# Attention scores as three rounded products of split queries and keys, in the softmax stages of a two-block network

## What is computed

```python
# first block, both layers: dilated attention, 8 heads of 64
scores = einsum(q, k) * d ** -0.5;  scores = where(mask, scores, -inf)
p = exp(scores - m);  o = einsum(p, v) / p.sum(-1)
# second block, second layer: differential attention, 4 heads with two maps of 64
attn = softmax(q1 @ k1 * s + bias_d) - lam * softmax(q2 @ k2 * s + bias_d);  out_d = attn @ v_d
# ... and chosen attention, 8 heads of 64 over the 256 best keys of a token, picked by an index score
out_c = softmax(where(chosen & causal, q @ k * s + bias_c, -inf)) @ v_c
```

## Time and profile before

| | |
|---|---|
| time, median of 3 runs | 3228.14 us (3226.29 to 3228.87) |
| profiled execution | 3228.16 us, of which 3226.3 us are the span of the instructions |
| PE busy | 2971.4 us (92%) |
| DVE busy | 2444.6 us (76%) |
| ACT busy | 1416.7 us (44%) |
| POOL busy | 420.5 us (13%) |
| dilated stages | 174.4 to 218.4 and 845.8 to 889.9 |
| differential, chosen stage | 2420.7 to 2483.4 and 2484.2 to 2556.0 |

### The profile page before, as it was taken

One profiled execution on the slowest core, in us unless ns is written; L12 is line 12 of the kernel. 1 busy time (PEld: TensorE's weight loads), 2 busy tenths in 40 slices (PEclk: granted clock), 3 DMA queues, 4 the chain that ended last, 5 costly groups with the idle time before them and its releaser, 6 DMA issues. The chain is left out here.

```text
span 3226.3 us, 40647 instructions
## 1 busy us (share of the span) xinstructions
PE 2971.4 (92%) x14002; PEld 2396.8 (74%) x14002; DVE 2444.6 (76%) x2663; ACT 1416.7 (44%) x1696; POOL 420.5 (13%) x249
## 2 busy tenths in 40 slices
PE   7998999999989999879979999995988979999995
PEld 6777788877777878656767888884765768888884
DVE  4566888565567996576978999996487669999996
ACT  1233211022323110163236777774336327777774
POOL 0110112211101213200000000001323100000001
PEclk9998999999989999989989999997999979999997
DMA  4242765332324663164239999994214249999994
GB/s 169 66 164 66 232 213 166 109 119 95 144 92 151 226 199 107 51 189 113 74 129 363 386 371 372 386 370 168 92 40 127 94 172 384 383 374 390 384 387 156
DMA packets 346603, 667.28 MB, mean 207 GB/s; under 512 B 21984, under 2 KB 138700, under 8 KB 338268
## 3 DMA queue, kind: packets, MB, share of 16 engines
q1 hardware_dynamic: 339708, 642.60, 56.5%
q0 software_dynamic: 6752, 22.81, 2.1%
HBM read 612.22 MB, written 53.13 MB: 206 GB/s over the span
## 5 line engine op out<-in xcount | busy, mean ns | idle before, releaser
L2924 DVE TENSOR_TENSOR expert_w_low<-expert_w_raw,expert_w_high 128x2048 fp32r<-128x2048 f32 x290 | 663.7, 2289 | 66.0 <-ACT expert_w_high L2881 65.7
L2881 ACT CAST expert_w_high<-expert_w_raw 128x2048 fp32r<-128x2048 f32 x290 | 555.0, 1915 | 192.1 <-PE bank L144 180.4
L142 PE MATMUL bank<-expert_w_high,expert_x_high 128*128 128x512 f32 x928 | 379.5, 409 | 6.5 <-DVE expert_w_low L2924 4.3
L142 PE MATMUL bank<-first_XH,first_w_high 128*128 128x512 f32 (+1 forms) x944 | 369.8, 392 | 0.0
L144 PE MATMUL bank<-expert_w_high,expert_x_low 128*128 128x512 f32 x928 | 365.3, 394 | 0.0
L143 PE MATMUL bank<-expert_w_low,expert_x_high 128*128 128x512 f32 x928 | 363.9, 392 | 0.0
L143 PE MATMUL bank<-first_XL,first_w_high 128*128 128x512 f32 (+1 forms) x944 | 363.1, 385 | 0.0
L144 PE MATMUL bank<-first_XH,first_w_low 128*128 128x512 f32 (+1 forms) x944 | 362.9, 384 | 0.0
L222 DVE TENSOR_TENSOR first_w_low<-first_w_raw,first_w_high 128x2048 fp32r<-128x2048 f32 (+2 forms) x94 | 287.1, 3054 | 3.2
L220 DVE CAST first_w_high<-first_w_raw 128x2048 fp32r<-128x2048 f32 (+2 forms) x94 | 111.7, 1188 | 173.1 <-PE bank L144 152.1
L1440 ACT ACTIVATE ffn_conv<-bank,ffn_taps 128x512 f32<-128x512 f32 x88 | 68.5, 780 | 358.4 <-PE bank L144 358.3
(11 more groups left out here) (545 smaller groups left out, 5962.1 us busy)
## 6 DMA issues: line engine op xcount, KB each, us to landing
expert_w_raw<-in_moe_w_gate_dram SPq DMA_DIRECT2D x116, 1024.0 KB, 8.4
expert_w_raw<-in_moe_w_up_dram SPq DMA_DIRECT2D x116, 1024.0 KB, 13.6
expert_w_raw<-in_moe_w_down_dram SPq DMA_DIRECT2D x58, 1024.0 KB, 13.9
modulation<-in_moe_w_down_dram SPq DMA_DIRECT2D x58, 1024.0 KB, 14.1
ffn_mod_w<-in_ada_w_dram SPq DMA_DIRECT2D x48, 1024.0 KB, 5.0
first_w_raw<-in_w_up_dram SPq DMA_DIRECT2D x88, 512.0 KB, 6.6
first_w_raw<-in_w_down_dram SPq DMA_DIRECT2D x22, 1024.0 KB, 4.8
first_w_raw<-in_w_in_dram SPq DMA_DIRECT2D x20, 1024.0 KB, 5.1
```

What stands on the lines that cost most here:

```text
L142: nc.tensor.matmul(out, rounded(st[0]), rounded(mv[0]), start=start, stop=False)
L2881: nc.scalar.copy(rounded(high[:, part_of(e, n), :]), weights.place(place)).then_inc(w_high, 1)
L2924: nc.vector.tensor_tensor(rounded(low[:, part_of(e, n), :]), weights.place(place), high[:, part_of(e, n), :], ALU.subtract).then_inc(w_spl ...
```

## The change

`ScoreParts` splits the queries and keys of a pair of heads: `round` casts both (128x512 each) on ACT, `rest` subtracts both on DVE, and `products` issues six fp32r products, alternating between the two heads' halves of the array. The first pair of the dilated stage and the first head of the differential stage keep the plain products. Each other pair is split a few units before it is used; the first pair of the chosen stage in unit 12 of the differential one. The low parts have two slots, so the two pairs whose low part has been overwritten are subtracted again (`AGAIN_AT`) and the last four units go through the pairs backwards. To make room, two of three slots of the chosen stage's bias rows move into the modulation tile, and the following phase's parts and rows move to `score_high` and to the mixed rows.

```diff
+class ScoreParts:
+    def round(self, act, h, done):
+        for n in range(2):
+            last = self.nc.scalar.copy(rounded(self.high(h)[n]), self.raw[n](h))
+        last.then_inc(done, 1)
+    def rest(self, dve, h, done):
+        for n in range(2):
+            last = self.nc.vector.tensor_tensor(rounded(self.low(h)[n]), self.raw[n](h), self.high(h)[n], ALU.subtract)
+        last.then_inc(done, 1)
+    def products(self, outs, h, width, queries, keys, stop):
+        high, low = self.high(h), self.low(h)
+        parts = ((high[0], high[1]), (high[0], low[1]), (low[0], high[1]))
+        for n, (q, k) in enumerate(parts):
+            for m, out in enumerate(outs):
+                r = width * m
+                done.append(self.nc.tensor.matmul(out, rounded(q[r:r + width, queries]), rounded(k[r:r + width, keys]), ...
...
 dilated_phase
+        SPLIT_AT = {0: 1, 2: 2, 5: 3}
...
+                if hp:
+                    pe.wait_ge(pair_split, hp)
+                    for last in parts.products(...)
...
                 for m in range(2):
                     softmax_max(i, m)
+                if i in SPLIT_AT:
+                    dve.wait_ge(pair_high, SPLIT_AT[i])
+                    parts.rest(dve, SPLIT_AT[i], pair_split)
                 if i >= 1:
                     copy(i - 1)
...
+                if i in SPLIT_AT:                       # ACT, after exp(i)
+                    parts.round(act, SPLIT_AT[i], pair_high)
                 if i >= 1:
                     copy(i - 1)
...
 chosen_attention_phase
+        SPLIT_AT = {3 * hp + 1: hp + 1 for hp in range(HEADS_C // 2 - 1)}     # units 1, 4, 7
+        AGAIN_AT = {units.index((hp + 2, TT - 1)): hp for hp in range(2)}     # units 13, 12
...
                 if i >= 1:
                     copy(i - 1)
+                if i in SPLIT_AT:
+                    dve.wait_ge(pair_high, SPLIT_AT[i])
+                    parts.rest(dve, SPLIT_AT[i], pair_split)
+                elif i in AGAIN_AT:
+                    parts.rest(dve, AGAIN_AT[i], pair_split)
...
 differential_phase
+        SPLIT_AT = {0: (parts, 1), 4: (parts, 2), 8: (parts, 3), 12: (next_parts, 0)}
...
                 if u >= 1:
                     weigh(u - 1)
+                if u in SPLIT_AT:
+                    which, h = SPLIT_AT[u]
+                    dve.wait_ge(head_high, split_number[u])
+                    which.rest(dve, h, head_split)
                 if u >= 2:
                     combine(u - 2)
```

More of the change, by code:

```diff
@@ L579, in _, with __init__, attn_score_parts @@
             V.tensor_tensor(S["KGR"][:, :], ps[k % BANKS][:, :], rest[:, :], ALU.mult).then_inc(gated, 1)
+class ScoreParts:
+    def __init__(self, nc, queries, keys, high, low):
+        self.nc, self.raw, self.high, self.low = nc, (queries, keys), high, low
+    def round(self, act, h, done):
[9 more added lines that the diff above has]
+        parts = ((high[0], high[1]), (high[0], low[1]), (low[0], high[1]))
+        done = []
+        for n, (q, k) in enumerate(parts):
+            for m, out in enumerate(outs):
+                r = width * m
+                done.append(self.nc.tensor.matmul(out, rounded(q[r:r + width, queries]), rounded(k[r:r + width, keys]),
+                                                  start=(n == 0), stop=stop and n == len(parts) - 1))
+        return done[-len(outs):]
+def attn_score_parts(nc, S, queries, keys):
+    high = lambda h: [S["score_high"][:, n, h, :] for n in range(2)]
+    low = lambda h: [S["score_low"][:, h % 2, n, :] for n in range(2)]
+    return ScoreParts(nc, lambda h: S[queries][:, h, :], lambda h: S[keys][:, h, :], high, low)
 def pair_values(V, k, h):
@@ L616, in dilated_phase @@
         zero_rows = G["consts"][:, 0:D]
+        rows_of = lambda a: (lambda hp: [a[:, 4 * n + hp, :] for n in range(2)])
+        parts = ScoreParts(nc, lambda hp: S["QA"][:, hp, :], lambda hp: S["KA"][:, hp, :], rows_of(G["XH"]), rows_of(G["XL"]))
+        pair_high = ph.sem("pair_high")
+        pair_split = ph.sem("pair_split")
+        SPLIT_AT = {0: 1, 2: 2, 5: 3}
         zero_set = ph.sem("zero_set")
@@ L3634, in chosen_attention_phase @@
         mix_bank = lambda i: ps[6 + i % 2]
+        parts = attn_score_parts(nc, S, "QC", "KC")
+        pair_high = ph.sem("pair_high")
+        pair_split = ph.sem("pair_split")
+        SPLIT_AT = {3 * hp + 1: hp + 1 for hp in range(HEADS_C // 2 - 1)}
+        AGAIN_AT = {units.index((hp + 2, TT - 1)): hp for hp in range(2)}
         block = ph.block()
@@ L3655, in scores @@
                 for m in range(2):
-                    r = HD_C * m
                     if i >= 2:
                         pe.wait_ge(max_done, 2 * (i - 2) + m + 1)
-                    nc.tensor.matmul(score_bank(i, m)[:, :], S["QC"][r:r + HD_C, hp, t * P:(t + 1) * P], S["KC"][r:r + HD_C, hp, :],
-                                     start=True, stop=False)
+                if t == TT - 1 and hp < 2:
+                    pe.wait_ge(pair_split, len(SPLIT_AT) + 2 - hp)
+                elif hp:
+                    pe.wait_ge(pair_split, hp)
+                parts.products([score_bank(i, m)[:, :] for m in range(2)], hp, HD_C, slice(t * P, (t + 1) * P), slice(0, SEQ), False)
                 if t == TT - 1:
@@ L3850, in scores @@
                         pe.wait_ge(max_done, 2 * (u - 2) + m + 1)
-                    nc.tensor.matmul(ps[2 * (u % 2) + m][:, :], S["QD"][r:r + HD_D, h, t * P:(t + 1) * P], S["KD"][r:r + HD_D, h, :],
-                                     start=True, stop=False)
+                    if h == 0:
+                        nc.tensor.matmul(ps[2 * (u % 2) + m][:, :], S["QD"][r:r + HD_D, h, t * P:(t + 1) * P], S["KD"][r:r + HD_D, h, :],
+                                         start=True, stop=False)
+                if h:
+                    pe.wait_ge(head_split, h)
+                    parts.products([ps[2 * (u % 2) + m][:, :] for m in range(2)], h, HD_D, slice(t * P, (t + 1) * P), slice(0, SEQ), False)
                 if u == 0:
@@ L3953, in _ @@
                                          accum_out=row_sum[:, u, m:m + 1]).then_inc(exp_done, 1)
+                if u in SPLIT_AT:
+                    which, h = SPLIT_AT[u]
+                    which.round(act, h, head_high)
                 if u >= 3:
@@ L4170, in second_block @@
         with ExitStack() as parts:
-            G["XH"], G["XL"] = parts.enter_context(nc.sbuf_tensor("attn_out_XH", [P, KD, SEQ], F32)), masks
-            rows = [chosen_bias.rows[:, r, :, :].rearrange("p m n -> p (m n)") for r in range(TT - 1)] + [S["Y"][:, TT - 1, :]]
+            G["XH"], G["XL"] = S["score_high"].rearrange("p r m n -> p (r m) n"), masks
+            rows = [S["Y"][:, r, :] for r in range(1, TT)] + [chosen_bias.own[:, :, :].rearrange("p m n -> p (m n)")]
             attn_out_phase(nc, G, S["Y"], w_out, mod(2), (S["QC"], rows, room[:, 3:5, :, :], S["VC"].rearrange("p m n -> p (m n)")), routers[1])
```

25 lines of the change are left out of this document (19 added, 6 removed).

## The result

3293.27 us, median of 4 runs (3288.64 to 3294.11), against 3228.51 us for the kernel before (4 runs): ratio 1.0201, interval 1.0189 to 1.0213. The change costs 65 us, where 26 were forecast; the sign was right, the size lies outside the range.

A forecast was written before the change was run, and what follows sets the result against it. DVE was taken to bind the differential stage and have little room in the chosen one, PE to bind the dilated ones. 9.6 + 6.6 + 9.0 + 1.0 = 26 us on 3228.16 gave 3254 us, range 3240 to 3268.

The forecast's parts named there:

- The bound: DVE full in the differential stage, 0.3 us a unit of room in the chosen; PE binds the dilated stages' steady part.
- the products take what was said: Scores on PE: six fp32r products run as three side-by-side pairs, 0.88 us instead of 1.06, gaining 0.18 us a unit.
- Rivals 1, 3 and 4: PE halves run serially: 3268 us, chance 0.10; DVE additions hide: 3222, 0.04; lags caught up within stages: about 3232, 0.07.
- Rival 2: PE's clock falls at each of some ten stalls, 1.7 us each: +15 us, about 3268 us; chance 0.11.
- One sentence: By the skill's weight-load rule the products' gain on PE would be nearly gone, which would not change the sum.
- Differential, +9.6 forecast: Differential stage: DVE idles 1.85 us and subtracts 1.22 us in units 4, 8 and 12, plus a start delay; +9.6 us.
- Chosen, +6.6 forecast: Chosen stage: DVE idles and subtracts 2.57 us in units 1, 4 and 7, plus a POOL meeting, less offsets; +6.6 us.
- Unit 4: Chosen stage: DVE's subtractions meet POOL's 4.54 us subtraction and wait for its end, 1.75 us more, less 0.8 us.
- the second meeting with POOL, which slides apart (0.5): Chosen stage: DVE's operation no longer meets POOL's second subtraction, taking 0.5 us off.
- DVE's delay reach PE at the mark: Chosen stage: the mark comes 7.1 us later; PE's wait for it grows from 0.85 to some 3 us.
- Dilated, +4.5 each forecast: Dilated stages: splits in units 0, 2 and 5 delay PE 5.2 us, products return 0.7; +4.5 each, both +9.0 us.
- Clock, +1 us forecast (bounds 0 to 6): Differential stage: splits leave PE idle some 2.3 us in a piece, a low clock follows; +1 us.

The follow-up runs named there:

- e2: Changed kernel without DVE's subtractions and waits for casts; all three products of a head take high parts, ACT casts behind its copy; 3227.8 us.
- e5: Changed kernel with unused filler fp32 products on PE in its longest stalls in all four stages; 3267.1 us.
- e13: Changed kernel with plain fp32 scores in both dilated stages, splits and their waits kept; 3275.8 us.
- e6: Changed kernel, but POOL zeroes the low parts of two output-weight slots in the chosen stage instead of subtracting them; 3273.5 us.
- e9: Changed kernel with DVE's subtractions a unit later and ACT's casts behind its copies, some dilated splits a unit later; 3253.3 us.
- after: The changed kernel itself, with all its splits and products, against the kernel before; 3293.27 us, ratio 1.0201.
- e12: Changed kernel with POOL's two output-weight subtractions in the chosen stage each cut into eight of 256 columns; 3279.0 us.
- e14: Changed kernel with plain fp32 scores in the first dilated stage only, splits kept; 3282.0 us.
- e15: Changed kernel with plain fp32 scores in the second dilated stage only, splits kept; 3273.9 us.

## Why the prediction fell short

The bound was read rightly: DVE's chain carries the splits in the full stages, and the products take what was said (0.89 for 0.88 us); nothing of it shows in the time (e2). Rivals 1, 3 and 4 are out by the rows above. Rival 2 named the right mechanism, with 15 us where at least 21 were; 3268 us is still short of 3293. One sentence is off by the prediction's own numbers: without the products' gain its sum would not stay as it is, but grow by 0.5 + 1.4 = 1.9 us. By steps:

- **Differential, +9.6 forecast, +14.2 measured.** DVE idled 1.73 us (1.85 said) and subtracted for 1.29. With PE filled the stage is at +10.6 (e5). The other 3.6 us are clock, as far as one can tell: the same code without fillers came as low as +11.7 (e13), with less low clock.
- **Chosen, +6.6 forecast, +16.9 measured.** Unit 4 behaved as said (2.40 us for the first subtraction). The step that failed here is "the second meeting with POOL, which slides apart (0.5)": it slid the other way, into nearly the whole of POOL's 4.53 us, and lost 3.55 us there where the kernel before had lost 0.53: 3.0 us more on DVE instead of 0.5 less. Without both blocks the stage is at +4.2 (e6). The path was wrong too. The prediction had DVE's delay reach PE at the mark, where PE waited 1.00 us and not 3, hardly more than the 0.85 before. PE stood 8.8 us instead in five waits before its turns, for a copy of ACT; in the two longest, 2.83 and 3.42 us, it came behind exponentials that had waited for DVE's late maximum.
- **Dilated, +4.5 each forecast, +15.8 and +18.2 measured.** On the good course of the clock it is +5.7 and +6.8 (e5), so this term was 1.2 and 2.3 us small, and 10.1 and 11.3 us are clock.
- **Clock, +1 us forecast (bounds 0 to 6).** This is the step that failed. In the four stages PE spent some 122 us at 0.50, by the length and the granted clock of each window (60.00 x 2 x 0.28 = 34 in the first), against 20 us before. The forecast counted a low stretch only behind the stalls of the differential stage and took its length from rows 15 (6.8 us). Stalls of 1.1 to 2.9 us were forecast for the dilated stages too (2.99 and 1.29 measured), but the clock was not asked about there, and there it stayed low for 17 and twice for 20.4 us. Fillers return 27 us over the four stages (e5), 2.3 of them in the chosen one, whose 12.7 us hold a further part.

9.6 + 6.6 + 9.0 + 1.0 = 26 became 14.2 + 16.9 + 34.0 = 65: of the 39 us missing, 21 to 25 are clock by e5's fillers in the dilated and differential stages (10.1 + 11.3, and up to 3.6), some 10 lie in the chosen stage, where e6 gives them to POOL's blocks and the clock behind them, and the rest lies in the dilated stalls.

Open: why the clock takes the one course or the other behind the same stall. Plain scores never took the long one in six profiled stages; what in the shorter products lets it is not shown. How the 12.7 us divide between waiting and clock wasn't tried either.

## What to carry to other kernels

Where PE is full and an edit makes it stand for 1 us or more, ask what the clock does there; its price here was at least 21 of 65 us. An operation that meets a long one of POOL costs by where it falls, so each delay ahead of it changes that price by up to POOL's whole operation: cut POOL's into pieces before adding work to DVE. And take the gain of cheaper products only where something waits for PE; place the split behind what others wait for (e9: 16 us of the first and 17 of the second dilated stage).

## What the runs showed of the hardware

- PE can be busy without a gap and stay at 1.2 GHz for 20.4 us (after, e6, e12, e14). The Trainium skill (TensorE: Matmul & The Clock Gate, What's actually happening) says that activity releases the throttle; here PE was active throughout and the clock stayed at 0.50 for a third of the stage (199.6 to 220.0 us of 174.7 to 234.7), while in e15 the same instructions had 1.00.
- More work on PE made the kernel faster: 14, 14, 28 and 30 more records in the four stages (e5) took 26 us off.
- Six fp32r products of 512 columns on the two halves of the array run in pairs, 0.89 us from the first start to the next product.
- Two operations of the two engines that block each other do so for one instruction: POOL's eight pieces of 0.73 us each let DVE's in between them (0.77 us instead of 3.90), and one of POOL's took 1.21 us beside DVE's subtractions (e12).
